# A fused four-layer block and diffusion block in fp32: sooner weight splits, idle matmuls in waits, and modulation units laid out by halves

## The chip, the cores and the metric

The kernel runs on one core of a Trainium2 chip, as one launch. The metric is device time in microseconds: the median of 3 runs was 1717.38 (1717.24 to 1717.69).

## The reference

The input x has 256 tokens of 1024 features. Everything is float32. A first block has four layers, each a mixer and a gated feed-forward network (FFN), both with residuals:

- layer 0: stick-breaking attention (16 heads); layer 1: chunked spatial gating; layer 2: a diagonal state-space scan (64 groups of 64 complex states) with a gated output; layer 3: attention again.
- each FFN: `h = rmsnorm(x) @ w_up` (1024 to 2 x 2816), a causal depthwise convolution over 3 tokens, `silu(g) * a`, and `@ w_down` (2816 to 1024).

A second block takes the result and a context of 256 tokens. Six vectors of 1024 come from `silu(c) @ w_mod + b_mod` (and from the context's own c); they shift, scale and gate. It has one layer: a mixer that joins latent attention and a gated linear recurrence in two directions, then a SwiGLU FFN of width 2816, and a final rmsnorm.

## The kernel before

Weights are streamed from HBM in units of 128 x 2048 floats (1 MB), 249 of them in one order (`PLAN`), through a ring of three raw buffers. A float32 product is made of three passes of a faster float format: each unit is split into a high part and a low part. `split_hi(s)` on ScalarE (ACT, L414) copies raw to whi, rounded; `split_lo(s)` on VectorE (DVE, L1020) writes wlo = raw - whi. Both parts have rings of three as well, so the high part of unit s waits until PE has used unit s-3, and the raw buffer is reloaded by SP's queue when wlo is written. TensorE (PE) makes for each pair of tiles `XH*whi`, `XL*whi`, `XH*wlo` (`product`, L1948 to L1950): 48 matmuls of 256 columns a unit.

All five instruction streams are written out by hand, in program order per engine, and meet by semaphores. `ahead(u)` issues the splits up to u+2 at the places where it stands; within the loops of an FFN the splits stand by hand.

An FFN has 33 units, numbered from u0: two up units, then ten times two up units and a down unit, and a last down unit. Up product j gives two tiles (a and g). On DVE `take(j)` (L1241) brings them from PSUM and scales them; ACT applies the last tap and the bias (L531, conv0); DVE adds two earlier taps (L1255, four instructions); ACT makes Silu (L536); DVE multiplies (L1262). After two products `hidden(h)` splits the pair (ACT L550, DVE L1276) for the down product h. PE's order is up 0, up 1, up 2, up 3, down 0, and then two ups and a down each time. In the FFNs 0 to 2 (`turned`) the last four ups come before the last three downs; in FFN 3 they do not, and the last down product follows one other down product. On DVE, FFN 1 has `matrices` and FFN 3 has `context_operand` between iterations (`aside`). The second block's FFN has no convolution (`conv=False`).

`scales()` makes the rms row of a fresh input: column sums on PE, root on ACT, reciprocal and a diagonal on DVE, a row of ones times it on PE (`row_sum`), and the copy RSTD (L1080). `scaled` (L1093) then takes products out of PSUM with that row. In attention(1), the first stage, units 0 to 2 are multiplied before the row is known.

In the state-space stage (from about 632 to 708 us of the span) DVE runs products, scans and rotations for eight steps s, GpSimd (POOL) part of the rotations, PE `inputs` (L2621), `own_pair` (L2634) and `outputs(s)` (L2661). Between these PE multiplies eight modulation units straight from raw: `modulation` (L1964), 32 float32 matmuls of 64 columns each into 32 rows of one PSUM bank; the profile has two records for each float32 matmul. `modulation_rows` (L1152) copies the bank, `modulation_turned` (L1975) turns it into vectors with four matmuls, and `modulated` (L1163) adds the bias. The glu units follow.

At the end of the second block's mixer PE waits for the last low parts of the operand (L1034), then runs two output units, two more with `sums` between them (L2113), and the FFN, whose first product waits for the normalised operand (`low` and L1054). Before the first product of the whole kernel there are 18 matmuls of 512 columns on a bf16 tile (L2702).

Of the kernel before, what the change touches and what calls it, by code (L numbers as in the profile page):

```python
# [23 lines left out]
P = 128  # L24
# [6 lines left out]
RING = 3  # L31
# [108 lines left out]
def program(nc, wst, mst, crow, vec, cst, xin, sgw, sgb, sbc, ctxin, ropes, out):  # L140
    with ExitStack() as ctx:
# [56 lines left out]
        MROW = AR[:, 2048:2560]  # L198
# [205 lines left out]
        def _(act):  # L404
# [112 lines left out]
            def ffn(layer, conv=True, aside=None, tail=None, then=None):  # L517
# [38 lines left out]
                for j in range(2):  # L556
                    ahead(u0 + j)
                    up(j)
# [453 lines left out]
        def _(dve):  # L1012
# [141 lines left out]
            def modulated(n, bank):  # L1154

                dve.wait_ge(S["mod_sum"], n + 1)
                dst = MODV[:, 16 * n:16 * n + 16, :].rearrange("p (x b a) r -> p b x a r", b=2, a=2)
                src = PS[:, bank, 0:32].rearrange("p (x a b r) -> p b x a r", a=2, b=2, r=2)
                add = VEC[:, VC["b_mod"] + 16 * n:VC["b_mod"] + 16 * n + 16].rearrange("p (x b a) -> p b x a", b=2, a=2)
                for half in range(2):  # L1160
                    r = slice(64 * half, 64 * half + 64)
                    for b in range(2):
                        ins = dve.tensor_tensor(dst[r, b ^ half], src[r, b],  # L1163
                                                add[r, b ^ half].unsqueeze(3).broadcast_to([64, 4, 2, 2]), ALU.add)
                ins.then_inc(S["mod_vec"], 1)
# [66 lines left out]
            def ffn(layer, conv=True, aside=None, then=None):  # L1232
# [11 lines left out]
                def up(j, it=None):  # L1244
                    k = 0 if it is None else it
                    bank = PS[:, 4 + (q0 + j) % 2, :].rearrange("p (a b) -> p a b", a=2)
                    if conv:

                        dve.wait_ge(S["conv0"], up0 + j + 1 + 2 * k)
                        for back in (1, 2):  # L1250
# [5 lines left out]
                            if back == 1:  # L1256
                                ins.then_inc(S["conv1"], 1)
                                dve.wait_ge(S["conv1"], up0 + j + 1 + 2 * k)
                            else:
                                ins.then_inc(S["conv2"], 1)  # L1260
                        dve.wait_ge(S["silu_ready"], up0 + j + 1 + 2 * k)
# [16 lines left out]

                if conv:
# [24 lines left out]
                if turned:  # L1304
                    s1 += 3 * (n - 2)
                    for h in (n - 1, n):
# [5 lines left out]
                        if conv and h == n:  # L1312
                            split_lo(s1 + 4)
                        hidden(h)
                    if not conv:
                        split_lo(s1 + 4)
                    split_lo(s1 + 5)
                else:
# [7 lines left out]
                    split_lo(s1 + 2)  # L1326
                t.s += 3 * n
# [29 lines left out]
            def attention(i):  # L1357
                scales()
# [182 lines left out]
            def state_space(i):  # L1541
# [90 lines left out]
                modulation_rows(0, 7)  # L1632
# [3 lines left out]
                for j in range(KT):  # L1636
                    ahead(t.u)
                    if j == 1:
                        modulated(0, 7)
# [302 lines left out]
        def _(pe):  # L1942
# [27 lines left out]
            def modulation_turned(n, bank):  # L1970

                pe.wait_ge(S["mod_rows"], n + 1)
                rows = ident.rearrange("p (q r) -> p q r", r=32)[:, :, 0:2]
                for c in range(4):
                    mm = pe.matmul(PS[:, bank, 8 * c:8 * c + 8], MROW[:, c * P:(c + 1) * P], rows,  # L1975
                                   start=True, stop=True)
                mm.then_inc(S["mod_sum"], 1)

# [191 lines left out]
            def ffn(aside=None, free=True, then=True, turned=True):  # L2170
# [61 lines left out]
                if turned:  # L2232
# [3 lines left out]
                    down(n - 1)  # L2236
                down(n, last=True)
# [96 lines left out]
            def last_mixer():  # L2334
# [227 lines left out]

                pe.wait_ge(S["op_lo"], t.op + 1)
# [19 lines left out]
                sums(2)  # L2583
                sums(3)

# [24 lines left out]
            def state_space():  # L2610
# [69 lines left out]
                modulation(0, 7)  # L2680
                for s in range(8):
                    if s < 7:
                        modulation(s + 1, 7)
# [8 lines left out]
                for mp in range(4):  # L2692
                    if mp:
                        features(at=T)
                    if mp == 0:
                        modulation_turned(0, 7)
# [239 lines left out]
```

## Time and profile before

| what | us |
|---|---|
| median of 3 runs | 1717.38 |
| the profiled execution | 1715.28 |
| its span | 1713.4 |
| PE busy / DVE busy / ACT busy | 1650.9 / 1239.6 / 852.7 |
| mean granted TensorE clock | 0.988 |

The span is that of the profiled execution, from its first to its last instruction. Busy times of engines overlap. The granted clock is 1.00 at 2.4 GHz and 0.50 at 1.2 GHz.

### The profile page before, as it was taken

How to read it: one execution, taken by the hardware profiler on the slowest of the kernel's cores; microseconds unless marked ns; L12 is line 12 of the kernel's file. 1: busy time of each engine (PE TensorE's matmuls, PEld its weight loads, DVE VectorE, ACT ScalarE, POOL GpSimd, SP SyncE). 2: the span in 40 equal slices, each digit the busy share in tenths (PEclk: the TensorE clock that was granted, in tenths of full speed). 3: DMA queues.
4: the chain of work that ended last, by engine and by line, in shares of the span. 5: the costliest groups of instructions: out<-in, count | busy, mean ns of one | idle time of the engine just before them, and what ended most of it. 6: DMA issues, size and time to landing. Idle time of an engine off the chain costs nothing.

```text
span 1713.4 us, 35193 instructions
## 1 busy us (share of the span) xinstructions
PE 1650.9 (96%) x14840; PEld 1581.9 (92%) x14840; DVE 1239.6 (72%) x1604; ACT 852.7 (50%) x979; POOL 104.6 (6%) x103
## 2 busy tenths in 40 slices
PE   9999999999999997899999999999999999899998
PEld 7989999999999996799999998999998779889998
DVE  6877777897878879857777786777766776654545
ACT  5465554656455541445555546555544644344343
POOL 1001000005400013100000000100000000000000
PEclk9999999999999998999999999999999999999999
DMA  8814555645455534454555781555552123145552
GB/s 324 326 51 171 183 185 176 216 149 188 161 183 183 173 121 150 150 172 151 193 174 176 278 318 65 185 174 178 187 172 99 71 78 99 48 151 187 179 181 90
DMA packets 40647, 286.82 MB, mean 167 GB/s; under 512 B 4640, under 2 KB 4640, under 8 KB 6496
## 3 DMA queue, kind: packets, MB, share of 16 engines
q1 hardware_dynamic: 39600, 280.99, 47.4%
q10 hardware_dynamic: 944, 4.33, 0.7%
q8 instruction: 81, 1.33, 0.3%
q14 instruction: 22, 0.18, 0.0%
HBM read 284.25 MB, written 1.05 MB: 167 GB/s over the span
## 4 chain that ended last, share of the span: by engine, by line
PE 68%; DVE 15%; ACT 9%; issue 7%; DVEq 0%; DMA 0%; ACTq 0%; SPq 0%
PE PS L1948 19%; PE PS L1949 19%; PE PS L1950 19%; ACT whi L414 5%; DVE AR L1255 4%; DVE wlo L1020 4%; ACT AR L531 2%; PE PS L1998 1%; PE PS L2291 1%; PE PS L2308 1%; PE PS L2621 1%; PE PS L2269 1%; PE PS L2661 1%; PE PS L2093 1%; PE PS L2438 0%
## 5 line engine op out<-in xcount | busy, mean ns | idle before, releaser
L1948 PE MATMUL PS<-XH,whi 128*128 128x256 f32 (+1 forms) x2792 | 808.8, 290 | 18.2 <-DVE wlo L1020 8.2
L1949 PE MATMUL PS<-XL,whi 128*128 128x256 f32 (+1 forms) x2792 | 800.5, 287 | 0.0
L1950 PE MATMUL PS<-XH,wlo 128*128 128x256 f32 (+1 forms) x2792 | 800.4, 287 | 0.0
L1020 DVE TENSOR_TENSOR wlo<-raw,whi 128x2048 fp32r<-128x2048 f32 x239 | 548.6, 2297 | 166.0 <-ACT whi L414 165.8
L1948 PEld LDWEIGHTS PS<-XH,whi 128*128 128x128 f32 x2792 | 537.8, 193 | 30.8 <-issue 15.1
L1949 PEld LDWEIGHTS PS<-XL,whi 128*128 128x128 f32 x2792 | 537.9, 193 | 3.7 <-issue 0.5
L1950 PEld LDWEIGHTS PS<-XH,wlo 128*128 128x128 f32 x2792 | 537.8, 193 | 3.3
L414 ACT ACTIVATE whi<-raw 128x2048 fp32r<-128x2048 f32 x239 | 454.4, 1902 | 58.9 <-PE PS L1950 48.9
L1948 PE MATMUL PS<-HH,whi 128*128 128x256 f32 x756 | 215.4, 285 | 8.8 <-DVE wlo L1020 7.0
L1949 PE MATMUL PS<-HL,whi 128*128 128x256 f32 x756 | 214.4, 284 | 0.0
L1950 PE MATMUL PS<-HH,wlo 128*128 128x256 f32 x756 | 214.3, 283 | 0.0
L1255 DVE SCALAR_TENSOR_TENSOR AR<-AR,VEC 128x255 f32<-128x255 f32 (+1 forms) x352 | 154.8, 481 | 14.3 <-ACT AR L531 4.7
L536 ACT ACTIVATE AR<-AR 128x256 f32<-128x256 f32 x88 | 36.7, 418 | 256.3 <-DVE AR L1255 256.3
L1948 PEld LDWEIGHTS PS<-HH,whi 128*128 128x128 f32 x756 | 145.0, 192 | 11.7 <-issue 8.2
L1950 PEld LDWEIGHTS PS<-HH,wlo 128*128 128x128 f32 x756 | 145.1, 192 | 0.2
L1949 PEld LDWEIGHTS PS<-HL,whi 128*128 128x128 f32 x756 | 145.1, 192 | 0.1
L531 ACT ACTIVATE AR<-AR,VEC 128x256 f32<-128x256 f32 x176 | 95.5, 590 | 79.6 <-DVE AR L1241 79.6
L2807 POOL TENSOR_TENSOR AR<-AR 128x512 f32<-128x512 f32 x21 | 46.1, 2196 | 785.2 <-ACT AR L470 771.8
L1241 DVE TENSOR_TENSOR AR<-PS,SM 128x512 f32<-128x512 f32 x88 | 60.5, 687 | 18.6 <-PE PS L1950 16.2
L1948 PE MATMUL PS<-whi,XH 128*128 128x256 f32 x256 | 73.0, 285 | 0.0
L1949 PE MATMUL PS<-wlo,XH 128*128 128x256 f32 x256 | 72.4, 283 | 0.0
L1950 PE MATMUL PS<-whi,XL 128*128 128x256 f32 x256 | 72.4, 283 | 0.0
(392 smaller groups left out, 1496.1 us busy)
## 6 DMA issues: line engine op xcount, KB each, us to landing
raw<-wst SPq DMA_DIRECT2D x247, 1024.0 KB, 4.9
AR<-mst SPq DMA_DIRECT2D x17, 1024.0 KB, 7.4
XT<-x_in SPq DMA_DIRECT2D x2, 512.0 KB, 5.4
raw<-wst SPq DMA_DIRECT2D x2, 512.0 KB, 6.4
AR<-crow ACTq DMA_DIRECT2D x2, 512.0 KB, 6.5
AR<-sbc ACTq DMA_DIRECT2D x1, 1024.0 KB, 6.2
AR<-ctxin ACTq DMA_DIRECT2D x1, 1024.0 KB, 5.8
y_out<-XT SPq DMA_DIRECT2D x4, 256.0 KB, 2.4
```

The costliest lines, as they stand in the source:

```text
L414: act.activation(whi[:, r, :], raw[:, u % RING, :], ACT.Copy).then_inc(S["w_hi"], 1)
L531: a = act.activation(CA[:, j % 2, i, :], UA[:, j % 2, i, :], ACT.Identity, bias=cb, scale=w2)
L536: act.activation(SG[:, j % 2, :], CA[:, j % 2, 1, :], ACT.Silu).then_inc(S["silu_ready"], 1)
L1020: dve.tensor_tensor(wlo[:, r, :], raw[:, u % RING, :], whi[:, r, :].bitcast(F32), ALU.subtract)\
L1241: dve.tensor_tensor(UA[:, j % 2], bank, RSTD.unsqueeze(1).broadcast_to([P, 2, T]), ALU.mult)\
L1255: ins = dve.scalar_tensor_tensor(y, UA[:, j % 2, i, 0:T - back], w, y, ALU.mult, ALU.add)
L1948: pe.matmul(dst, sh, mh, start=first, stop=False, **kw)
L1949: pe.matmul(dst, sh, ml, start=False, stop=False, **kw)
L1950: return pe.matmul(dst, sl, mh, start=False, stop=last, **kw)
L1998: mm = pe.matmul(PS[:, b, m * T:(m + 1) * T], stat[:, k * 256 + m * P:k * 256 + m * P + P], mov[:, k, 0:T], start=first and (m, k) == (0, ...
L2093: mm = pe.matmul(PS[:, 6, c:c + 1], SQ[:, i, c * P:(c + 1) * P], ones[:, 0:1], start=(i == 0), stop=(i == tiles[-1]))
L2807: ins = pool.tensor_tensor(SQ[:, 0:2, :], SQ[:, 0:2, :], SQ[:, 2 * mp:2 * mp + 2, :], ALU.add)
```

## The change

It has four parts. In each convolution FFN the split of unit u0+3 is made before the work on product 0, that of u0+4 within it, and all later splits stand one unit earlier. In attention(1) DVE makes its fourth split before it waits for `row_sum`. `idle(n)` puts n matmuls of 512 columns on a bf16 tile into PSUM bank 7, unread, at four places: before the last down product of FFN 3 (6), before the wait for the operand's low parts in the second block (11), and before and after its last sums (5 and 9). A modulation unit has 16 float32 matmuls of 128 columns, for two halves of the columns and two halves of the contraction, in two PSUM banks; the turning has 8 matmuls with a 4-column selector that also adds the two contraction halves.

```diff
-        MROW = AR[:, 2048:2560]
+        MROW = AR[:, 2048:3072]
+        SEL = SM[:, 256:260]
...
@@ scalar, ffn
-                for j in range(2):
-                    ahead(u0 + j)
-                    up(j)
+                if conv:
+                    ahead(u0 + 1)
+                    up(0, beside=t.s)
+                    t.s += 1
+                    up(1)
+                else:
+                    for j in range(2):
+                        ahead(u0 + j)
+                        up(j)
...
                             split_hi(s1 + 2 * (h - n + 1) + j)
-                            up(2 * h + j, beside=s1 + 4 if conv and h == n and j else None)
+                            up(2 * h + j)
                         hidden(h)
+                    split_hi(s1 + 4)
                     if not conv:
-                        split_hi(s1 + 4)
-                    split_hi(s1 + 5)
+                        split_hi(s1 + 5)
                 else:
...
                     hidden(n)
-                    split_hi(s1 + 2)
-                t.s += 3 * n
+                t.s += 3 * n - (1 if conv else 0)
...
@@ vector
-            def modulation_rows(n, bank):
-                dve.tensor_copy(MROW, PS[:, bank, :]).then_inc(S["mod_rows"], 1)
+            def modulation_rows():
+                a, b = (ident[:, 64 * h:64 * h + 64].rearrange("p (c r) -> p c r", r=32)[:, :, 0:2] for h in range(2))
+                dve.tensor_tensor(SEL.rearrange("p (c r) -> p c r", r=2), a, b, ALU.add)
+                dve.tensor_copy(MROW.rearrange("p (a b) -> p a b", a=2), PS[:, 6:8, :]).then_inc(S["mod_rows"], 1)
...
+            def modulated():
+                dve.wait_ge(S["mod_sum"], 1)
+                add = VEC[:, VC["b_mod"]:VC["b_mod"] + 16]
+                dve.tensor_tensor(MODV[:, 0:16, :], PS[:, 7, 0:32].rearrange("p (j r) -> p j r", r=2),
+                                  add.unsqueeze(2).broadcast_to([P, 16, 2]), ALU.add).then_inc(S["mod_vec"], 1)
...
@@ vector, ffn: up(j) is now convolve(j) and gated(j)
                 if conv:
                     scales()
-                for j in range(2):
-                    if conv:
-                        take(j)
-                    ahead(u0 + j)
-                    up(j)
+                    take(0)
+                    ahead(u0 + 1)
+                    convolve(0)
+                    take(1)
+                    split_lo(t.s)
+                    t.s += 1
+                    gated(0)
+                    up(1)
+                else:
+                    for j in range(2):
+                        ahead(u0 + j)
+                        up(j)
...
                             up(2 * h + j)
-                        if conv and h == n:
-                            split_lo(s1 + 4)
                         hidden(h)
+                    split_lo(s1 + 4)
                     if not conv:
-                        split_lo(s1 + 4)
-                    split_lo(s1 + 5)
+                        split_lo(s1 + 5)
                 else:
...
                     hidden(n)
-                    split_lo(s1 + 2)
-                t.s += 3 * n
+                t.s += 3 * n - (1 if conv else 0)
...
             def attention(i):
-                scales()
+                def fourth():
+                    split_lo(t.s)
+                    t.s += 1
+                scales(fourth if i == 1 else None)
...
@@ tensor
-            def modulation(g, bank):
+            def modulation(g):
                 pe.wait_ge(w_loaded[t.u % RING], 16 * (t.u // RING + 1))
-                for k in range(KT):
-                    for c in range(4):
-                        r, o = 32 * (c ^ (g % 2)), P * (g // 2) + 64 * (c % 2)
-                        mm = pe.matmul(PS[r:r + 32, bank, o:o + 64], SCP[:, k, :],
-                                       raw[:, t.u % RING, k * 256 + 64 * c:k * 256 + 64 * c + 64],
-                                       start=(k == 0), stop=(k == KT - 1))
+                for k in range(4):
+                    for h in range(2):
+                        for c in range(2):
+                            r, o, kh = 64 * h + 32 * c, P * (g % 4), 4 * h + k
+                            mm = pe.matmul(PS[r:r + 32, 6 + g // 4, o:o + P], SCP[:, kh, :],
+                                           raw[:, t.u % RING, kh * 256 + P * c:kh * 256 + P * c + P],
+                                           start=(k == 0), stop=(k == 3))
...
+            def modulation_turned():
+                pe.wait_ge(S["mod_rows"], 1)
+                for g in range(8):
+                    mm = pe.matmul(PS[:, 7, 4 * g:4 * g + 4], MROW[:, g * P:(g + 1) * P], SEL, start=True, stop=True)
                 mm.then_inc(S["mod_sum"], 1)
+            def idle(n):
+                for _ in range(n):
+                    pe.matmul(PS[:, 7, :], IDB[:, :], IDB[:, :].unsqueeze(1).broadcast_to([P, 4, P]),
+                              start=True, stop=True)
...
                     down(n - 1)
+                else:
+                    idle(6)
                 down(n, last=True)
...
+                idle(11)
                 pe.wait_ge(S["op_lo"], t.op + 1)
...
                 sums(2)
+                idle(5)
                 sums(3)
+                idle(9)
```

## Rows read from the trace of the kernel before

**Rows 1.** The page: busy time and its share of the span, and the last chain.
```profile
PE 1650.9 (96%) x14840; PEld 1581.9 (92%) x14840; DVE 1239.6 (72%) x1604; ACT 852.7 (50%) x979; POOL 104.6 (6%) x103
...
PE 68%; DVE 15%; ACT 9%; issue 7%; DVEq 0%; DMA 0%; ACTq 0%; SPq 0%
```

**Rows 2.** Waits of the whole kernel: us in total, times, longest.
```profile
DVE wlo L1020 <- ACT whi L414: 165.8, 143, 7.5
...
PE PS L1948 <- DVE wlo L1020: 15.2, 33, 1.4
```

**Rows 3.** Timeline of FFN 0's start: start, length, instruction, [idle before it, releaser].
```profile
149.00 1.90 ACT L414 ACTIVATE whi<-raw 128x2048 fp32r<-128x2048 f32 x1
...
156.40 1.90 ACT L414 ACTIVATE whi<-raw 128x2048 fp32r<-128x2048 f32 x1
...
146.85 1.79 DVE L1255 SCALAR_TENSOR_TENSOR AR<-AR,VEC 128x255 f32<-128x255 f32 x4 [1.16 <-ACT AR L531]
...
150.93 2.29 DVE L1020 TENSOR_TENSOR wlo<-raw,whi 128x2048 fp32r<-128x2048 f32 x1 [0.78 <-ACT whi L414]
...
160.77 0.36 PE L1948 MATMUL PS<-HH,whi 128*128 128x256 f32 x1 [1.41 <-DVE wlo L1020]
```

**Rows 4.** PE's waits in four stretches: 134:329.5, 411:605, 764:958, 1088:1261 us.
```profile
PE PS L1948 <- DVE wlo L1020: 2.3, 4, 1.4
...
PE PS L1948 <- DVE wlo L1020: 4.7, 10, 1.4
...
PE PS L1948 <- DVE wlo L1020: 2.5, 4, 1.4
...
PE PS L1948 <- DVE wlo L1020: 4.4, 11, 1.4
```

**Rows 5.** Stretches: length, busy PE PEld DVE ACT POOL, granted clock, DMA.
```profile
30.45:33.86 3.41, 3.41 (x18) 3.41 (x18) 3.41 (x3) 0.00 (x0) 0.00 (x0) 0.50 0.87 341
...
1484.50:1487.90 3.40, 2.83 (x13) 2.87 (x14) 3.24 (x3) 1.76 (x2) 0.00 (x0) 0.50 0.02 5
...
1511.80:1515.20 3.40, 3.40 (x17) 3.40 (x17) 3.40 (x10) 2.16 (x5) 0.00 (x0) 0.51 0.00 0
```

**Rows 6.** Timeline of attention(1)'s start, ACT, DVE and PE.
```profile
21.59 1.92 ACT L414 ACTIVATE whi<-raw 128x2048 fp32r<-128x2048 f32 x1
...
25.71 0.42 DVE L1080 COPY SM<-PS 128x256 f32<-128x256 f32 x1 [2.44 <-PE PS L2099]
26.16 0.69 DVE L1093 SCALAR_TENSOR_TENSOR AR<-PS,SM 128x512 f32<-128x512 f32 x1
...
29.71 0.39 PE L1948 MATMUL PS<-XH,whi 128*128 128x256 f32 x1 [2.13 <-DVE AR L1093]
```

**Rows 7.** A stretch of FFN 0's loop, columns as in rows 5.
```profile
200.00:300.00 100.00, 100.00 (x836) 100.00 (x835) 74.83 (x95) 50.53 (x58) 0.00 (x0) 1.00 0.54 181
```

**Rows 8.** Timeline of the end of FFN 3, ACT and PE.
```profile
1257.42 1.09 ACT L531 ACTIVATE AR<-AR,VEC 128x256 f32<-128x256 f32 x2 [2.56 <-DVE AR L1241]
...
1269.92 0.39 PE L1948 MATMUL PS<-HH,whi 128*128 128x256 f32 x1 [1.75 <-DVE HL L1276]
```

**Rows 9.** Timeline of the state-space stage and the turning, PE and DVE.
```profile
648.66 2.10 PE L2621 MATMUL PS<-AR 32*128 32x128 f32 x64
...
653.36 0.59 PE L2661 MATMUL PS<-AR 128*32 128x64 f32 x27 [1.04 <-issue]
...
653.79 1.11 PE L1964 MATMUL PS<-raw,SM 128*32 128x64 f32 x62
...
654.12 0.69 DVE L1563 TENSOR_TENSOR AR<-PS,AR 128x512 f32<-128x512 f32 x1 [2.40 <-PE PS L2661]
...
714.67 0.96 PE L1975 MATMUL PS<-CST,AR 128*128 128x8 f32 x8
```

**Rows 10.** Timeline of the second block before its FFN, PE.
```profile
1485.07 0.55 PE L1948 MATMUL PS<-XH,whi 128*128 128x256 f32 x1 [3.55 <-DVE XL L1034]
...
1507.81 1.13 PE L2113 MATMUL PS<-AR,CST 128*128 128x256 f32 x4 [1.40 <-ACT AR L428]
...
1511.62 0.37 PE L1948 MATMUL PS<-XH,whi 128*128 128x256 f32 x1 [2.69 <-DVE XL L1054]
```

More of the change, by code:

```diff
@@ L1148, in norm_stream @@
                     dve.tensor_tensor(x, x, RSTX.unsqueeze(1).broadcast_to([P, 2, T]), ALU.mult).then_inc(S["normed"], 1)
-            def modulation_rows(n, bank):
-                dve.tensor_copy(MROW, PS[:, bank, :]).then_inc(S["mod_rows"], 1)
[L1154 to L1165, printed above, removed]
+            def modulation_rows():
[7 more added lines that the diff above has]
+                                  add.unsqueeze(2).broadcast_to([P, 16, 2]), ALU.add).then_inc(S["mod_vec"], 1)
             def modulated_gain(i):
@@ L1242, in take, with convolve @@
                         .then_inc(S["pp_taken"], 1)
-                def up(j, it=None):
+                def convolve(j, it=None):
                     k = 0 if it is None else it
-                    bank = PS[:, 4 + (q0 + j) % 2, :].rearrange("p (a b) -> p a b", a=2)
                     if conv:
@@ L1260, in up, with gated @@
                                 ins.then_inc(S["conv2"], 1)
+                def gated(j, it=None):
+                    k = 0 if it is None else it
+                    bank = PS[:, 4 + (q0 + j) % 2, :].rearrange("p (a b) -> p a b", a=2)
+                    if conv:
                         dve.wait_ge(S["silu_ready"], up0 + j + 1 + 2 * k)
@@ L1277, in hidden, with up @@
                         .then_inc(S["hl_ready"], 1)
+                def up(j, it=None):
+                    convolve(j, it)
+                    gated(j, it)
                 if conv:
                     scales()
-                for j in range(2):
-                    if conv:
-                        take(j)
-                    ahead(u0 + j)
-                    up(j)
+                    take(0)
[10 more added lines that the diff above has]
+                        up(j)
                 hidden(0)
@@ L1631, in state_space @@
                 dve.wait_ge(S["w_used"], sum(MODS[0]))
-                modulation_rows(0, 7)
+                modulation_rows()
                 lows(3)
@@ L1638, in state_space @@
                     if j == 1:
-                        modulated(0, 7)
+                        modulated()
                         dve.wait_ge(S["mod_vec"], 1)
@@ L1956, in x @@
                 return XH[:, k, a:b], XL[:, k, a:b]
-            def modulation(g, bank):
+            def modulation(g):
                 pe.wait_ge(w_loaded[t.u % RING], 16 * (t.u // RING + 1))
-                for k in range(KT):
-                    for c in range(4):
-                        r, o = 32 * (c ^ (g % 2)), P * (g // 2) + 64 * (c % 2)
-                        mm = pe.matmul(PS[r:r + 32, bank, o:o + 64], SCP[:, k, :],
-                                       raw[:, t.u % RING, k * 256 + 64 * c:k * 256 + 64 * c + 64],
-                                       start=(k == 0), stop=(k == KT - 1))
+                for k in range(4):
[5 more added lines that the diff above has]
+                                           start=(k == 0), stop=(k == 3))
                 mm.then_inc(S["w_used"], 1)
                 t.u += 1
[L1970 to L1976, printed above, removed]
+            def modulation_turned():
+                pe.wait_ge(S["mod_rows"], 1)
+                for g in range(8):
+                    mm = pe.matmul(PS[:, 7, 4 * g:4 * g + 4], MROW[:, g * P:(g + 1) * P], SEL, start=True, stop=True)
                 mm.then_inc(S["mod_sum"], 1)
+            def idle(n):
+                for _ in range(n):
+                    pe.matmul(PS[:, 7, :], IDB[:, :], IDB[:, :].unsqueeze(1).broadcast_to([P, 4, P]),
+                              start=True, stop=True)
             def fresh_bank():
@@ L2679, in state_space @@
                 pe.wait_ge(S["silu_c"], 1)
-                modulation(0, 7)
+                modulation(0)
                 for s in range(8):
                     if s < 7:
-                        modulation(s + 1, 7)
+                        modulation(s + 1)
                     if s % 2 == 0:
@@ L2695, in state_space @@
                     if mp == 0:
-                        modulation_turned(0, 7)
+                        modulation_turned()
                     features(at=T)
```

## The prediction

> **What bounds the kernel now.** I read the page first. The matmul engine is busy 1650.9 us of a 1713.4 us span, and the chain that ended last lies 68% on it [rows 1]. So the kernel runs at TensorE's pace, and a change of this kind can win only in two places: where PE stands still, and where it runs at half its granted clock. The list of waits names the standing: across the whole kernel PE waits 15.2 us in 33 pieces for the split that VectorE (DVE) makes (L1020, which writes wlo), and DVE in turn waits 165.8 us for ScalarE's (ACT) half of the split, L414 [rows 2]. The timeline of the first FFN shows the pattern: a split is 1.90 us on ACT, then 2.29 us on DVE, in series; ACT begins its halves (149.00, 156.40) only when the work on the previous product is done, DVE follows, and PE stands 1.41 us before its first down product [rows 3]. The waits by stretch put 2.3, 4.7, 2.5 and 4.4 us of this into the four convolution FFNs, 13.9 us in all, the largest piece of each being 1.4 [rows 4]. The rows by stretch with the granted clock then show what a long wait costs afterwards: 0.50 or 0.51 for some 3.4 us, which is 1.2 GHz instead of 2.4 [rows 5].
>
> **Attention(1), the fourth split.** DVE stands idle 2.44 us for row_sum, then scales, splits unit 3, scales; PE needs the second scale and resumes at 29.71 after 2.13 us [rows 6]. ACT's half of unit 3 ends at 23.51, so the moved split runs at about 23.5 to 25.8, inside the idle time. DVE then copies RSTD (0.42) and scales twice (0.69 each, with overlap 1.3): 27.65. PE's previous work ends at 29.71 - 2.13 = 27.58. Gain 2.06 us. Behind that wait PE runs 3.41 us at clock 0.50 [rows 5]; without the wait nothing is idle for the clock to fall on: half of 3.41 = 1.7 us more. Sum **3.75**; bounds 2.06 (the clock falls anyway) and 3.75. The earlier split also frees its raw slot earlier, and the loads behind it on SP's queue start sooner, so I charge nothing there.
>
> **FFN starts and the whole loop.** Unit u0+3 is now split before the first product's work, u0+4 in the middle of it, and every later split of the FFN stands one unit earlier. A unit is 48 matmuls; 836 in 100 us make it 5.74 us [rows 7]. Counted back from 160.77 - 1.41, PE ends u0+3 at 159.4, u0+2 at 153.4 and u0+1 at about 147.4. ACT's half of u0+3 can follow its table load, 142.7 to 144.6; DVE's follows the take, 145.7 to 148.0 (before: 150.93 to 153.22). ACT's half of u0+4 needs the slot that PE leaves at 147.4, so it ends at 149.3; DVE convolves product 0 (1.79), takes product 1, and splits u0+4 until about 152.7 (before: 160.6). The hidden pair is then ready at about 157, as before. PE, without its two waits, reaches the down product at about 159: no wait, and some six microseconds of lead stay. What is queued behind the new waits: in the loop ACT's half now waits for the unit that PE has only just finished, and behind it on ACT stand the convolution bias, Silu and the hidden copy. Per product that serial chain is 1.90 + 2.29 + 1.79 + 0.8 = 6.8 us [rows 3], and one iteration (two products, a down split, the hidden pair) comes to about 17.5 us, against PE's 3 x 5.74 = 17.2. It is as long only while the lead is full; once some is used up ACT's waits are over early and DVE's busy 13 us remain (74.83 of 100 us [rows 7]), so it should not stall PE. All 13.9 us could go; in FFN 1 and 3 DVE has other work between iterations which may use up the lead, so I take 4.3 of 4.7 and 4.0 of 4.4: **13.1** (bounds 5.7, the four first waits alone, and 13.9). At the ends of FFN 0 to 2 a split leaves the path of the hidden pair, but PE has two down products to do meanwhile: nothing.
>
> **End of FFN 3.** Here the last down product follows more directly, and PE already waits 1.75 us for the hidden pair [rows 8]. Now ACT's half before product 20 needs the unit that PE ends at about 1256.6; before, it was done ahead of it. ACT's bias step moves from 1257.42 [rows 8] to 1256.6 + 1.90 = 1258.55, and what hangs behind it (DVE's split, four convolutions, then product 21's same chain, whose half waits for PE again) ends about 1.3 us later. PE's wait becomes some 3.0 us: **-1.3** (bounds 0 and -2).
>
> **Modulation units.** Each has half as many matmuls of twice the columns. 62 records of 64 columns took 1.11 us, 17 ns apart; 64 of 128 columns took 2.10 us, 33 ns [rows 9]. A unit is 64 x 17 = 1.10 us now and 32 x 33 = 1.05 then: PE saves next to nothing by streaming. The Trainium skill, TensorE: Matmul & The Clock Gate, Back-to-back issue gap, states that starts never lie closer than about 25 ns however few the columns; by that a unit would fall from 1.6 to about 1 us, but the row has 17 ns, so the row decides. What remains is the number of instructions, 8 x 32 x 2 = 512 matmul and load records less. In the outputs PE stands 1.04 us at 653.36 with no releaser ("issue"), and DVE, which is on the path in this stage, waits 2.40 us for exactly those outputs [rows 9]. With 64 matmul records fewer ahead of it that stall should go. I take **+1.0**; bounds -0.5 (the stall moves to a worse place) and +2.4 (all of DVE's wait). The Trainium skill, Runtime: NRT & Kernel Launch, Instruction fetch mechanics, calls crossing a block of 256 instructions mostly hidden; by that the term is 0. The turning has 8 matmuls for 4: those 8 records took 0.96 us [rows 9], 0.8 of it before the next start, so 8 more cost **-0.8**, on PE, with the glu units behind them. DVE's copy before it doubles from 0.7 to some 1.3 us plus 0.2 for SEL, ahead of the last low part; PE needs that only after 36 products, 4.3 us, which hides it; without that cover it would cost 0.8.
>
> **Fillers.** A 512-column matmul costs at most two 256-column ones of 0.12, so 0.24, an estimate from rows 7's count. 11, 5, 9 and 6 of them are 2.6, 1.2, 2.2 and 1.4 us, and stand before waits of 3.55, 1.40, 2.69 [rows 10] and 1.75 [rows 8]: they fit, and the waits, which DVE and ACT set, keep their ends. But the clock behind them, 0.50 over 2.83 us of busy PE and 0.51 over 3.40 [rows 5], should stay high: 1.4 + 1.5 (the second is partly paced by DVE) = **2.9**; bounds 0 and 3.1. If the clock were low already, a filler would take 0.43 us and 11 of them overrun the wait by 1.2.
>
> **Sum.** 3.75 + 13.1 - 1.3 + 1.0 - 0.8 + 2.9 = 18.65 us. The profiled execution took 1715.28, 1.9 more than its span; the median of the runs is 1717.38, 2.1 above it. I take the gain off the median: **1698.7 us**, a ratio of 0.989. The forecast's own range is 1695.5 to 1702: FFN term +0.8, state space +1.4, and 1.7 us for each stretch of half clock that comes or goes.
>
> **Rivals.** (A) *The lead is used up at once* (chance 0.13). ACT's waits in the loop are for PE's latest unit; the small waits of 0.3 to 0.5 us inside the loops stay, and only the four first ones go, 5.7 for 13.1: 7.4 less, 1706. For it: 17.5 against 17.2 us; against it: DVE's quarter of idle time in the loop. (B) *Fillers leave the clock as it was* (0.10): 1701.6. For it: PE still idles before each wait ends. (C) *The state-space stage gives nothing, or its stall moves* (0.07): 1700. (D) *It gives all of DVE's wait* (0.05): 1697.3. (E) *Slower* (0.02): the loop's serial chain, which now contains a wait for PE, becomes the period. There are some 34 iterations; above 18.65/34 = 0.55 us each it turns the sign, at 0.7 it costs 23.8 and gives 1722.5. Against it: the chain shortens as soon as PE has waited once. My forecast has 0.63.
>
> **Chances.** The range 1694.5 to 1704 leaves out A, E and tails: 2 in 10. A measurement tells 0.2%, 3.4 us, from no change; every case but E lies beyond that: faster 0.97, same 0.01, slower 0.02.
>
> **What would show it.** The first down product of each FFN follows without a gap; PE's wait for wlo falls from 15.2 us to about 2; unit 3 of attention(1) starts near 27.7; the last down product of FFN 3 waits about 3 us; DVE's 2.40 us wait becomes about 1.3; the clock stays 1.00 behind the filled waits; PE's matmul records fall by 256 - 8 - 31 = 217. I am wrong if the loops show regular waits of PE, if half clock appears in new places for more than 10 us in sum, or if weight loads come late once they are asked for sooner.

## The result and the profile after

The kernel after took 1703.32 us (median of 4 runs, 1701.9 to 1704.36) beside 1717.31 (1716.21 to 1717.69) for the kernel before on the same chip: a ratio of 0.9919, 95% interval 0.9902 to 0.9936, 14.0 us faster. The prediction was 1698.7 us, a gain of 18.65, with a range of 1694.5 to 1704.0. So direction and range held, near the upper end of the range, and a quarter of the gain is missing; the measured time lies nearer to rival A's 1706 than to the forecast. The profiled execution took 1704.35 us over a span of 1702.4.

The page of the kernel after, its busy times and its last chain, as in [rows 1]:

```profile
PE 1649.9 (97%) x14623; PEld 1581.2 (93%) x14623; DVE 1237.9 (73%) x1602; ACT 853.9 (50%) x979; POOL 105.8 (6%) x103
...
PE 65%; DVE 18%; ACT 9%; issue 6%; DMA 1%; DVEq 0%; ACTq 0%; SPq 0%
```

PE's records fell by 217, as forecast, but DVE's share of the chain rose from 15% to 18%. In the waits of the whole kernel (total, times, longest) PE's 15.2 us for wlo [rows 2] are nearly gone, and another wait, for the hidden pair (HL, XL), has grown:

```profile
DVE wlo L1026 <- ACT whi L415: 181.3, 154, 7.5
...
PE PS L1965 <- DVE HL L1282: 6.7, 6, 4.1
...
PE PS L1965 <- DVE XL L1282: 2.9, 1, 2.9
...
PE PS L1965 <- DVE wlo L1026: 2.3, 5, 0.9
```

Where the time came from is read by one instruction of DVE, the copy of RSTD at the head of each stage (L1080 before, L1086 after), and by the first and last XT additions. Each column below is how much sooner the event comes after than before, in us, and what the stage so ended gained:

| event | before | after | sooner | gain in between |
|---|---|---|---|---|
| FFN 0 starts | 144.54 | 140.96 | 3.6 | 3.6, attention(1) |
| gating starts | 341.82 | 335.77 | 6.05 | 2.5, FFN 0 |
| FFN 1 starts | 416.23 | 410.18 | 6.05 | 0 |
| state space starts | 621.15 | 616.88 | 4.3 | **-1.8, FFN 1** |
| glu ends | 757.38 | 751.94 | 5.4 | 1.2, state space and turning |
| attention(7) starts | 964.07 | 956.01 | 8.1 | 2.6, FFN 2 |
| FFN 3 starts | 1084.70 | 1076.63 | 8.1 | 0 |
| second block's norm ends | 1297.31 | 1288.80 | 8.5 | 0.4, FFN 3 |
| first XT addition of its output units | 1489.48 | 1479.69 | 9.8 | 1.3 |
| span ends | 1713.40 | 1702.43 | 11.0 | 1.2 |

The spans differ by 11.0 us, the medians by 14.0; below, single executions of one kernel differ by more than 2 us, so stages are compared in traces and whole kernels by ratios.

In FFN 1 the waits were 4.7 us for wlo before [rows 4]. After, none of that is left, and this is there (waits of PE, 405 to 600 us):

```profile
PE PS L1965 <- DVE XL L1282: 2.9, 1, 2.9
PE PS L1965 <- DVE HL L1282: 1.6, 2, 1.0
PE PS L1965 <- DVE AR L1243: 1.1, 1, 1.1
```

5.6 us in place of 4.7. DVE's timeline, first and last instruction of FFN 1 up to its last hidden pair, in the kernel before:

```profile
416.23 0.42 DVE L1080 COPY SM<-PS 128x256 f32<-128x256 f32 x1 [1.42 <-PE PS L2099]
...
597.77 0.68 DVE L1276 TENSOR_TENSOR XL<-AR,XH 128x512 fp32r<-128x512 f32 x1
```

and after, with PE's last down product behind it:

```profile
410.18 0.42 DVE L1086 COPY SM<-PS 128x256 f32<-128x256 f32 x1 [1.43 <-PE PS L2121]
...
591.50 0.69 DVE L1282 TENSOR_TENSOR XL<-AR,XH 128x512 fp32r<-128x512 f32 x1 [0.70 <-ACT XH L551]
...
592.25 0.58 PE L1965 MATMUL PS<-XH,whi 128*128 128x256 f32 x1 [2.87 <-DVE XL L1282]
```

From first to last it is 181.5 us before and 181.3 after. From the third pair of products on, DVE's steps from the first `take` of a pair to that of the next are as long in both kernels: 19.8, 16.2, 19.1, 16.2, 18.4, 16.2 and 18.1 us. PE stands less at the front of FFN 1, but DVE and ACT need the same time for their work, and PE meets them at the last hidden pair. In the kernel before the pair was written at 598.45, and PE came to it at about 598.9, when the down product before it was through:

```profile
593.18 0.36 PE L1948 MATMUL PS<-XH,whi 128*128 128x256 f32 x1 [0.29 <-DVE wlo L1020]
```

So only some 0.5 us could be won there. FFN 1 went at DVE's pace before the change already, and the waits on wlo only hid it.

FFN 1 did not only win nothing, it lost. From the start of the last hidden pair to the start of the last XT addition it is 9.1 us before and 10.5 after: DVE's next split now waits 1.11 us for ACT's high part, which ACT makes only after its half of the pair, where before it was made ahead of it. The other 0.7 us lie behind the last XT addition.

One iteration of that loop after, DVE:

```profile
531.03 0.69 DVE L1243 TENSOR_TENSOR AR<-PS,SM 128x512 f32<-128x512 f32 x1 [0.22 <-DVE AR L1469]
531.64 2.28 DVE L1026 TENSOR_TENSOR wlo<-raw,whi 128x2048 fp32r<-128x2048 f32 x1
533.84 1.90 DVE L1256 SCALAR_TENSOR_TENSOR AR<-AR,VEC 128x255 f32<-128x255 f32 x4
536.22 0.42 DVE L1268 TENSOR_TENSOR AR<-AR 128x256 f32<-128x256 f32 x1 [0.48 <-ACT AR L537]
536.56 0.69 DVE L1243 TENSOR_TENSOR AR<-PS,SM 128x512 f32<-128x512 f32 x1
538.02 2.29 DVE L1026 TENSOR_TENSOR wlo<-raw,whi 128x2048 fp32r<-128x2048 f32 x1 [0.78 <-ACT whi L415]
540.23 1.90 DVE L1256 SCALAR_TENSOR_TENSOR AR<-AR,VEC 128x255 f32<-128x255 f32 x4
542.61 0.42 DVE L1268 TENSOR_TENSOR AR<-AR 128x256 f32<-128x256 f32 x1 [0.48 <-ACT AR L537]
544.41 2.29 DVE L1026 TENSOR_TENSOR wlo<-raw,whi 128x2048 fp32r<-128x2048 f32 x1 [1.38 <-ACT whi L415]
546.62 0.68 DVE L1282 TENSOR_TENSOR HL<-AR,HH 128x512 fp32r<-128x512 f32 x1
```

and the ACT instructions that two of its waits are for:

```profile
542.16 0.42 ACT L537 ACTIVATE AR<-AR 128x256 f32<-128x256 f32 x1 [3.19 <-DVE AR L1256]
542.49 1.90 ACT L415 ACTIVATE whi<-raw 128x2048 fp32r<-128x2048 f32 x1
```

The next take begins at 547.23, so the period is 547.23 - 531.03 = 16.2 us, of which 0.48 + 0.78 + 0.48 + 1.38 = 3.1 are waits for ACT, 2.2 of them for high parts. None is for PE. ACT stands idle 3.19 us before Silu and only then makes the high part, 1.90, for which DVE waits 1.38. PE's period, from one down product (530.20) to the next (547.48), is 17.3 us, so DVE makes up 1.1 us in an iteration without `matrices`, while the four iterations with `matrices` are 18.1 to 19.8 us from take to take.

### The profile page after: what moved, and what is told of

Same layout as the page of the kernel before. It is cut to its first block, busy times and chain, and to the rows that moved or that the text cites. A ratio compares the mean times of both kernels' runs of the same rounds, so it can differ in the third digit from the quotient of the medians.

```text
span 1702.4 us, 34735 instructions
## 1 busy us (share of the span) xinstructions
PE 1649.9 (97%) x14623; PEld 1581.2 (93%) x14623; DVE 1237.9 (73%) x1602; ACT 853.9 (50%) x979; POOL 105.8 (6%) x103
## 4 chain that ended last, share of the span: by engine, by line
PE 65%; DVE 18%; ACT 9%; issue 6%; DMA 1%; DVEq 0%; ACTq 0%; SPq 0%
PE PS L1965 19%; PE PS L1966 18%; PE PS L1967 18%; ACT whi L415 6%; DVE wlo L1026 6%; DVE AR L1256 4%; ACT AR L532 1%; PE PS L2315 1%; PE PS L2332 1%; PE PS L2293 1%; DVE HL L1282 1%; DMA raw<-wst 1%; DVE AR L1602 1%; PE PS L2115 1%; DVE AR L1243 1%
## 5 line engine op out<-in xcount | busy, mean ns | idle before, releaser
L1026 DVE TENSOR_TENSOR wlo<-raw,whi 128x2048 fp32r<-128x2048 f32 x239 | 550.4, 2305 | 181.4 <-ACT whi L415 181.3
L1268 DVE TENSOR_TENSOR AR<-AR 128x256 f32<-128x256 f32 x88 | 37.5, 426 | 40.6 <-ACT AR L537 40.6
```

What stands on the lines that cost most here:

```text
L1026: dve.tensor_tensor(wlo[:, r, :], raw[:, u % RING, :], whi[:, r, :].bitcast(F32), ALU.subtract)\
L1268: dve.tensor_tensor(HID[:, j % 2, :], CA[:, j % 2, 0, :], SG[:, j % 2, :], ALU.mult)\
```

## The experiments

Whole kernels are given as ratios to the kernel before on the same chip. First the parts of the change alone, and the change without its idle matmuls.

**b_ffn_splits**, the kernel before with the FFN hunks of the diff only (ACT's and DVE's `ffn`).

> The kernel before with the sooner FFN splits alone. By the prediction's terms (FFN starts and loops 13.1, end of FFN 3 -1.3) it gains 11.8 us on the kernel before: about 1705.5 us, each FFN 2.3 to 4.3 us shorter but FFN 3 2.7. By the theory read from the trace after (the lead is spent at the hidden pair before the last down product; FFN 1 ends later, not sooner): FFN 0 and FFN 2 gain 2.3 to 2.5 each, FFN 1 loses 1.8 and FFN 3 gains 0.4, in all 3.4 us: about 1713.9 us, with waits of 2 to 3 us for the hidden pair before the last down product of FFN 1 and about 4 us in FFN 3.

Measured: ratio 0.9977 (0.9968 to 0.9986), 3.9 us. By the RSTD copies, FFN 0 gained 2.5, FFN 2 2.6, FFN 1 lost 0.9, and FFN 3 with the norm behind it gained 0.1, PE's wait before its last down product growing to 5.40 us without the idle matmuls. The last hidden pair of FFN 1 comes 595.36 - 414.03 = 181.3 us after its start, again. This is the second theory's number, 3.4, not the prediction's 11.8.

**b_fourth**, the kernel before with the split in `attention(1)` only.

> The kernel before with the fourth split of attention(1) alone. By the prediction's term the first stage ends 3.75 us sooner (2.06 of wait, 1.7 of half clock) and the whole kernel too: about 1713.6 us. A rival: the time is given back at the end of FFN 0, where the hidden pair comes late: then the end of FFN 0 moves by less than 2 us and the whole by less than 2.

Measured: ratio 0.9991 (0.9982 to 1.0), 1.5 us. Attention(1) ends 3.2 us sooner, with no half clock behind it; FFN 1 ends 3.15 sooner, so nothing is given back at the ends of FFN 0 and FFN 1. The whole kernel did not gain the 3.75 us of the prediction, which lie outside the interval (0 to 3.1 us). The state-space stage of the profiled execution takes 3.4 us longer than before, though PE's program is that of the kernel before. The rival was right in that part of the gain was lost and wrong in the place. Whether the stage took it back or only scattered, one execution does not show; its scatter is taken up below.

**b_modulation**, the kernel before with the modulation hunks only.

> The kernel before with the modulation units and the turning of the change alone. By the prediction's terms (+1.0, -0.8) it gains 0.2 us. By the trace after, the state-space section is 2.1 us shorter and the turning 0.9 longer: 1.2 us, about 1716.1. A rival: the 2.1 us belong to the whole change, by where the ring of weights stands after FFN 1, and this kernel gains nothing or loses 0.9.

Measured: ratio 0.9989 (0.998 to 0.9998), 1.9 us. In the trace it gained 2.0 up to the first XT addition behind the state space, and the glu section with the longer turning lost 0.9. The interval leaves out zero and, by a little, the prediction's 0.2 us, so the gain belongs to the part itself; its size is loose.

**a_no_idle**, the kernel after without the four `idle(...)` lines.

> The kernel after without its four runs of idle matmuls. By the prediction's term the half clock comes back behind the waits of the second block and the kernel is 2.9 us slower than after. By rival B the clock does as it did and the time is that of after. By the trace after, 2.4 us: 1.3 before the output units, 1.1 before the last FFN, and nothing in FFN 3, where the clock falls behind the 4.08 us wait with or without the 6 matmuls.

Measured: ratio 0.9956 (0.9942 to 0.9969), 0.0037 or 6 us slower than after. The half clock is back behind both waits. Two stretches of a_no_idle, columns as in [rows 5], the granted clock third from the end:

```profile
1476.10:1479.60 3.50, 3.02 (x14) 3.05 (x15) 3.23 (x3) 1.68 (x2) 0.00 (x0) 0.51 0.00 0
1503.50:1506.90 3.40, 3.40 (x18) 3.40 (x17) 3.40 (x9) 2.26 (x5) 0.00 (x0) 0.51 0.00 0
```

and after, where the same work runs at full clock:

```profile
1477.00:1480.00 3.00, 3.00 (x28) 3.00 (x27) 2.77 (x3) 0.76 (x1) 0.00 (x0) 1.00 0.00 0
1503.00:1506.00 3.00, 3.00 (x25) 2.92 (x24) 3.00 (x9) 1.95 (x4) 0.00 (x0) 1.00 0.00 0
```

From FFN 3's start to the end the two profiled executions differ by 3.5 us: 1.0 in FFN 3 and 2.5 behind its norm. The stretch from that norm to the end shows the worth of the fillers of the second block by itself. It takes 413.6 to 413.7 us in every kernel that has them; without them it takes 416.1 to 416.3 where the half clock behind each of the two waits lasts 3.4 us (before, b_fourth, a_no_idle), and 417.9 to 418.1 where it lasts 6.8 (b_ffn_splits, b_modulation, b_beside). The medians differ by more than the two traces do, and the profiled execution of a_no_idle was its fastest with its highest mean granted clock, 1706.93 us at 0.989; the other four have 0.981 to 0.988 and took 1707.84 to 1712.61.

The four ratios together (0.0023, 0.0009, 0.0011, 0.0037) make 0.0080, the change 0.0081: the parts add, as far as intervals of about 0.001 each can tell.

Next, why FFN 1 and FFN 3 gave so little. The theory is the one above: DVE's side work and ACT's order set their pace. The rival is that the place of the splits itself costs at the end.

**a_no_matrices**, the kernel after with `matrices` left out, so that the state-space stage works on buffers of zeros:

```diff
-                if p == 0:
+                if p < 4:
                     return
+                if p == 4:
+                    dve.memset(AR[:, B0 + 7168:B0 + 8192], 0.0).then_inc(S["s5_mats"], 1)
+                    return
```

> The kernel after, with the state-space matrices that DVE computes between the iterations of FFN 1 left out (their buffers hold zeros). If DVE's side work is what spends FFN 1's lead, the waits of 1.05, 0.50, 1.12 and 2.87 us in FFN 1 go, the half clock at 591.6 to 598.4 too, and FFN 1 ends about 8 us sooner than after (5.5 of waits, some 3 of clock), by more than the 1.8 us that it had lost. If the order of splits alone does it, the waits stay within 1 us of what they are and FFN 1 ends at most 1 us sooner.

Measured: one run, 1697.65 us. FFN 1 ends 7.1 us sooner than after, by the XT additions and its start. PE's waits in it:

```profile
PE PS L1968 <- DVE XL L1068: 0.6, 2, 0.4
```

The last hidden pair starts 174.45 us after FFN 1's start and no half clock follows. Without the side work the lead is not used up.

**a_beside**, the kernel after with ACT's high parts moved in front of Silu in the loops (and the second one of each tail iteration likewise); nothing on DVE or PE is touched:

```diff
                         with act.Fori(0, e - b) as it:
+                            split_hi(s1 + 3 * b, it)
                             for j in range(2):
-                                split_hi(s1 + 3 * b + j, it)
-                                up(2 + 2 * b + j, it)
-                            split_hi(s1 + 3 * b + 2, it)
+                                up(2 + 2 * b + j, it, beside=s1 + 3 * b + 1 + j if conv else None)
+                                if not conv:
+                                    split_hi(s1 + 3 * b + 1 + j, it)
                             hidden(1 + b, it)
...
```

> The kernel after, with ACT's high parts inside the loops of the convolution FFNs, and the second of each tail iteration, issued between the convolution bias and Silu, no longer behind Silu. By the serial-chain theory DVE's idle times of 0.78 and 1.38 us per iteration (16.2 us of DVE's chain against PE's 17.2) go, DVE makes up for its side work in FFN 1 and 3, the waits of FFN 1 fall from 5.5 us in sum to about 1, its half clock goes, and the wait before the last down product of FFN 3 falls from 4.08 us: 6 to 9 us gained on after in the two FFNs, none in FFN 0 and 2. By the rival, high parts that come earlier wait for PE's slots in front of Silu, DVE's work on the hidden pair comes later, and the FFNs are as long or longer.

Measured: 1690.28 us, ratio 0.9845 (0.9831 to 0.9858), some 13 us less than after. In its trace FFN 1 gained 7.2 us, FFN 3 with the norm behind it 4.1, FFN 0 0.2 and FFN 2 0.2; another 2.4 lies between FFN 1 and the glu units, where the program is the same, and is no more than that stage scatters by. The waits of PE in FFN 1:

```profile
PE PS L1969 <- DVE XL L1072: 0.4, 1, 0.4
```

and DVE in an iteration of FFN 1:

```profile
531.20 0.43 DVE L1272 TENSOR_TENSOR AR<-AR 128x256 f32<-128x256 f32 x1 [1.44 <-ACT AR L537]
531.54 0.68 DVE L1247 TENSOR_TENSOR AR<-PS,SM 128x512 f32<-128x512 f32 x1
532.14 2.28 DVE L1030 TENSOR_TENSOR wlo<-raw,whi 128x2048 fp32r<-128x2048 f32 x1
...
540.47 0.69 DVE L1247 TENSOR_TENSOR AR<-PS,SM 128x512 f32<-128x512 f32 x1 [0.28 <-PE PS L1971]
```

The wait for ACT before the split is gone (531.54 to 532.14), and DVE now has to wait for PE's product at 540.47: it has caught up. The rival's cost shows too, 1.44 us before L1272 where 0.48 was, because the high part stands in front of Silu; but it arises only once DVE is up to date, and PE does not feel it. While DVE was late, right behind side work, it waited 0.48 us before L1272 and took 13.9 us from take to take (457.67 to 471.53), near the 13 us that the prediction had expected.

**b_beside**, the same edit in the loops of the kernel before.

> The kernel before with ACT's high parts in front of Silu in the loops of the convolution FFNs, and the old places of the first splits. If the sooner first splits are needed for the gain, the four waits of 1.4 us stay and only the small ones in FFN 1 and FFN 3 go (4.7 - 1.4 and 4.4 - 1.4, so up to 6.3 us). If DVE's serial chain was what mattered all along, this kernel alone gains as much as the sooner splits with it, 13 us on after's 3.9 us for the splits, and is near 1700.

Measured: 1704.71 us, ratio 0.9926 (0.9913 to 0.994), 12.7 us: nearly as much as the whole change gained. FFN 0 and FFN 2 gained 1.2 and 1.3, FFN 1 4.9, FFN 3 and the norm 3.8. From the start to the last hidden pair of FFN 1 it is 591.79 - 415.19 = 176.6 us. PE's waits up to 634 us, then from 757 to 1262:

```profile
PE PS L1949 <- DVE wlo L1021: 4.5, 7, 1.4
...
PE PS L1949 <- DVE wlo L1021: 3.5, 5, 1.4
```

The four waits of 1.4 us stay, one in each FFN, as the first theory has it, but the gain is twice what it allowed and well short of the 16.9 us that the second asked: both were half right. The order on ACT, not the place of the splits, was the greater part, and the sooner splits are needed only for the first down products.

**a_tail3**, the kernel after with the split of the unit behind FFN 3 made after the last hidden pair (`split(s1)` before `up(2 * n)`, `split(s1 + 1)` behind `hidden(n)`, on ACT and DVE).

> The kernel after, with the split of the first unit behind FFN 3 made after the hidden pair of its last down product instead of before it. DVE's chain before that product is shorter by 1.9 to 3.1 us (a split of 2.29 us and a wait of 0.78 go, the convolution bias then sets the time), so the wait falls from 4.08 to 1 to 2.2 us; if the granted clock then stays at 1.00, 1.7 us more: 2 to 4 us gained on after. Rival: what follows the FFN waits for the later split and gives it all back, gain below 1.

Measured: ratio 0.9908 (0.9892 to 0.9923), not to be told from after by itself, where 2 to 4 us were expected. In the trace PE's wait is

```profile
1254.71 0.48 PE L1968 MATMUL PS<-HH,whi 128*128 128x256 f32 x1 [2.24 <-DVE HL L1283]
```

in place of 4.08, and FFN 3 with the norm behind it is 1.8 us shorter. Nothing is given back (from the last XT addition of FFN 3 to the end it is 435.0 us in both), but 3.4 us of half clock still follow the 2.24.

**a_fill**, the kernel after with `idle(10)` before the last down product of FFN 1 and `idle(18)` for `idle(6)` in FFN 3.

> The kernel after with 10 idle matmuls before the last down product of FFN 1 (a wait of 2.87 us) and 18 in place of 6 in FFN 3 (4.08 us and 1.4 of idle matmuls). If a standing PE is what lets the granted clock fall, the stretches of half clock behind both go: 3.4 us (6.8 at half clock) in FFN 1 and 1.7 in FFN 3, about 5 us gained, while the waits end when they did. If the clock falls for another reason, no change.

Measured: ratio 0.9918 (0.9905 to 0.9932), as after. The end of FFN 1, 592.0 to 598.4 us, after and then in a_fill:

```profile
592.00:598.40 6.40, 6.15 (x29) 6.15 (x30) 4.60 (x6) 4.50 (x5) 0.00 (x0) 0.50 0.29 95
```

```profile
592.00:598.40 6.40, 5.91 (x49) 5.91 (x50) 4.71 (x6) 4.75 (x5) 0.00 (x0) 1.00 0.31 93
```

The clock does stay at 1.00 and PE runs 49 records where it ran 29, yet the last XT addition ends at 602.67 after and at 602.69 in a_fill. DVE's split, the four XT additions 2.1 us apart and the low parts between them set the time there; PE then waits 0.37 and 0.36 us between pairs. The state-space stage began 0.9 us sooner, measured from FFN 1's start. In FFN 3, where PE sets the pace, the fillers gave 1.5 us. So fillers do keep the clock up, as the first of the two expectations has it, but the 3.4 us that were to come of it in FFN 1 did not come, since DVE sets the end there.

**a_mod_pieces**, the kernel after with two 64-column matmuls for each 128-column one of the modulation units:

```diff
-                for k in range(4):
+                for e, k in ((0, 0), (0, 1), (0, 2), (0, 3), (64, 0), (64, 1), (64, 2), (64, 3)):
...
-                            r, o, kh = 64 * h + 32 * c, P * (g % 4), 4 * h + k
+                            r, o, kh = 64 * h + 32 * c, P * (g % 4) + e, 4 * h + k
...
```

> The kernel after with each 128-column matmul of the modulation units made as two of 64 columns, as many instructions as before the change, in the new layout (two contraction halves, two banks). The stretch from the row of rstd before the state-space stage to its first XT add took 94.6, 96.2 and 98.0 us in kernels with the old units and 90.4 to 92.6 in seven with the new. If the number of instructions does it, this one is back at 94 to 98 and 2 to 4 us slower than after; if the layout or the order of banks does it, it stays at 90.4 to 92.6.

Measured: 1707.44 us, ratio 0.9948 (0.9934 to 0.9961), 5 us slower than after. From the RSTD copy to the first XT addition behind the state space it takes 94.8 us. The four kernels with the old units took 94.6, 95.1, 96.2 and 98.0 (mean 96.0); the eight others with the new units, c_both_idle aside, 90.4 to 93.6 (mean 92.1). PE's idle time with the releaser "issue" in that stage is 7.7 to 11.4 us with the old units, 11.3 here, and 3.6 to 9.4 with the new. The rows here:

```profile
PE PS L2688 <- issue: 6.1, 4, 3.7
...
PE PS L1982 <- issue: 3.6, 3, 2.8
...
PE PS L2661 <- issue: 1.6, 1, 1.6
```

So the layout and the two banks are not what gained: with them kept, the time goes back. It goes with the number of instructions, and with their width, which no run here changes alone. One execution of each kernel and a scatter of 3 us leave the size loose: 2 us in this trace against after, 4 by the two means, 5 by the ratios, for 256 records.

**c_both**, a_beside and a_tail3 together, the fastest kernel here.

> The kernel after with both edits that gained: ACT's high parts in front of Silu, and the split behind FFN 3 made after its hidden pair. With the high parts alone PE still waits 1.84 us before the last down product of FFN 3 and runs 3.4 us at half clock behind it. If the two shorten the same chain one after the other, the wait goes to about 0 and the half clock too: 2 to 3.5 us less than with the high parts alone, which ran in 1690.3 us. If they share the same time (the bias and PE's last up product set the chain once it is short), under 1 us.

Measured: 1688.49 us, ratio 0.9836 (0.9822 to 0.9849), 28 us less than before and 14 less than after. PE's wait before the last down product of FFN 3 is 0.2 us, where it was 1.84 in a_beside and 2.24 in a_tail3. FFN 3 is 3.1 us shorter than in a_beside up to its last XT addition, but 6.8 us of half clock follow, and with the norm it is 1.6; the ratios of the two overlap. So the wait went, as the first of the two expectations has it, and the half clock did not. Its last chain:

```profile
PE 84%; DVE 9%; ACT 4%; issue 2%; DMA 1%; SPq 0%; DVEq 0%; ACTq 0%
```

68% of it lay on PE before, 65% after; now it is 84%.

**c_both_idle**, c_both with `idle(13)` before the first modulation unit.

> As the one with both edits, and 13 idle matmuls before the first modulation unit, where PE waits 3.6 us and then runs 3.4 us or 6.8 us at half clock. If PE's clock matters there: 1.7 us or more gained. If that stage goes at DVE's pace, as the end of FFN 1 did, where a clock that stayed high gained 0.6 us or less: nothing.

Measured: ratio 0.9853 (0.9838 to 0.9869), 0.0017 above c_both; the two intervals overlap. The expected 1.7 us did not come. The stage is 1.0 us longer in the trace, less than its scatter:

```profile
630.98 4.58 PE L2005 MATMUL PS<-IDB 128*128 128x512 bf16 x13 [2.78 <-DVE AR L1104]
...
635.50 1.95 PE L1989 MATMUL PS<-raw,SM 128*32 128x128 f32 x64
```

Most of the wait, 2.78 us, lies in front of the fillers, since another wait stands there; the clock had fallen to 0.50 at 630.9, the fillers took 0.35 us each, and the modulation unit began at 635.50 though its operand was there at 631.6 (ACT L721 ran from 631.35 for 0.22). So here the filler would have to stand in front of the first of the waits; no run tries that.

## Why the prediction was right in sum and wrong in the FFNs

- **Attention(1), 3.75.** 3.6 us after and 3.2 alone, with the wait at 0.42 us and no half clock behind it. The step held in its stage; of the whole kernel b_fourth moved only 1.5 us (0 to 3.1).
- **FFN starts and loops, 13.1.** All four first waits went, and FFN 0 and FFN 2 gave 2.5 and 2.6 for 2.3 and 2.5 forecast. FFN 1 gave -1.8 (-0.9 in b_ffn_splits) for 4.3. The step that failed: "once some is used up ACT's waits are over early and DVE's busy 13 us remain". DVE's waits of 3.1 us an iteration are for Silu and for ACT's high parts queued behind it, and stay however late DVE is; its period does not fall to 13 but to 16.2, and recovers 1.1 us an iteration against 17.3. a_beside takes 7.2 us out of FFN 1 by changing only that. The doubt stood in the text ("may use up the lead") and was priced at 0.4 us for each of FFN 1 and FFN 3.
- **Ends of FFN 0 to 2, nothing.** True for FFN 0 and FFN 2. In FFN 1 PE's 2.87 us wait for the hidden pair is the place where the lost gain came out, and the high part that now stands behind the pair on ACT cost 1.1 us more.
- **End of FFN 3, -1.3.** The wait became 4.08 us, not 3.0, and 5.40 without the fillers, so the term was 3.65 and not 1.3 us of standing. I had worked out only ACT's wait for its slot. The split of the next stage's unit now stood in the chain before the hidden pair; moving it takes 1.84 us off the wait (a_tail3). ACT's order takes 2.24 off it (a_beside), and both leave 0.2 (c_both). That FFN 3's `context_operand` had made DVE late, as `matrices` did in FFN 1, fits but is not shown: no run leaves it out. FFN 3 gave 0.4 in all for 2.7.
- **Modulation, +1.0 and -0.8.** 2.1 and -0.9 in the trace, 3.9 and -0.9 by the means of all kernels. The mechanism, fewer instructions, fits a_mod_pieces; the term was sized by the one "issue" wait of the profile before, 1.04 us, where others of 1.8 and 2.5 us stood in the same stage. The Trainium skill, Runtime: NRT & Kernel Launch, Instruction fetch mechanics, calls the crossing of a block of instructions mostly hidden, by which the term would be 0. Here 3.6 to 9.4 us of idle time without a releaser remain in the stage after the change, and the term is above 0; that this idle time is fetching, no run shows. The working "from 1.6 to about 1 us" takes 25 ns for the old units and a row's 33 ns for the new; the term does not use it.
- **Fillers, 2.9.** 3.5 us in the traces and 6 by the ratios. The clock stayed at 1.00 behind both waits of the second block, worth 2.5 us in the traces, so rival B fell. In FFN 3, for which the 2.9 had nothing, it did not stay: 3.4 us at 0.50 follow the 4.08 us wait, 6.8 without the fillers, and the six matmuls were worth 1.0 us. The size was off because the half clock behind the second block's waits lasts 3.4 us in some executions and 6.8 in others, where the fillers are worth 4.2 to 4.5 us.
- **Rivals.** A, that the lead is used up at once, came true in FFN 1 and 3 alone, by DVE's chain and not by waits on PE; no regular waits of PE showed. For the FFNs it was the nearest all the same: by A they give 5.7 - 1.3 = 4.4 us, and b_ffn_splits measured 3.9.

- **Signs.** The first down products follow at once, PE's wait for wlo fell to 2.3 us, unit 3 of attention(1) starts at 27.64, and the records fell by 217, all as forecast. DVE's wait of 2.40 us became 2.05, not 1.3. Of the signs of being wrong one came, just: in the profiled execution half clock stands in new places for 10.2 us, 6.8 at the end of FFN 1 (591.6 to 598.4 us) and 3.4 at that of FFN 3 (from 1260.6).

By the ratios the FFNs gave 7.9 us less than forecast and attention(1) 2.3 less, the fillers 3.4 more and the modulation units 1.7 more. The sum came out in range by luck, because these errors had both signs.

## What to carry to other kernels

When a wait is taken out of an engine's stream, measure from the start of the stage to the last product that the other engine has to deliver: if that length is what it was, the gain will come out again as a wait at the end. When an in-order engine waits for an input and has ready work queued behind that wait, ready work that another engine needs goes in front of it, even at the price of delaying the waiting step a little. A filler or a higher clock was worth something only where PE is the engine that the next step waits for, and 13 fillers placed behind a first wait came when the clock had already fallen.

## What the runs showed of the hardware that was not expected

- The half clock behind one and the same wait is not of one length: behind the 3.55 us wait in the second block it lasted 3.4 us before, in b_fourth and in a_no_idle, and 6.8 in b_ffn_splits, b_modulation and b_beside.
- The eleven idle matmuls did not stand inside the wait that they shortened. They ran from 1467.07 to 1469.61 us, ahead of product matmuls whose operands were ready; these ended 2.3 us later for it, the wait behind them shrank from 3.56 (a_no_idle) to 1.18 us, the wait ended at the same time, and the clock stayed at 1.00.
- A wait of 1.75 us at the end of FFN 3 left the clock at 1.00 before and was followed by 3.4 us of half clock in b_beside.
- The state-space stage, with the same instructions on every engine, took 90.4 to 93.6 us from one kernel to another, with 3.6 to 9.4 us of PE's idle time under "issue". What sets where these fall stays open.
- An idle matmul of 512 columns took 0.23 us at full clock (11 in 2.54) and 0.35 where the clock was 0.50 for the first 3.3 us of them (13 in 4.58).
